# A flat loop over passes in TensorE's expert program, its three bodies in another order, and two small matmuls moved into the first gather

## The reference, cut to what matters

```python
def moe_ffn(h, w_router, b_router, w_exp_in, b_exp_in, w_exp_out, b_exp_out):
    logits = (t @ w_router + b_router).astype(jnp.float32)       # t: 256 x 1024, 32 experts
    top_val, top_idx = lax.top_k(logits, TOP_K)                  # 4 of 32
    gate_w = jax.nn.softmax(top_val, axis=-1)
...
        hb = xb @ w_exp_in[e] + b_exp_in[e]                      # 1024 -> 2 x 1024
        g = jnp.minimum(hb[:, :D_FF_2], SWIGLU_LIMIT)
        u = jnp.clip(hb[:, D_FF_2:], -SWIGLU_LIMIT, SWIGLU_LIMIT)
        a = g * jax.nn.sigmoid(SWIGLU_ALPHA * g) * (u + 1.0)
        return a @ w_exp_out[e] + b_exp_out[e]                   # 1024 -> 1024
...
    y = jnp.einsum('nk,nkd->nd', gate_w, y_slot)
```

## Time and profile before

| | before |
|---|---|
| runs, us | 1498.84, 1501.26, 1500.84 |
| median, us | 1500.84 |
| profiled execution, us | 1501.09 |
| its span, us | 1499.2 |
| granted TensorE clock, mean | 0.98 |
| experts | from about 550 us to the end |

### The profile page before, as it was taken

How to read it: one execution, slowest core, us unless ns; L and a number is a source line. 1 busy time by engine, 2 the same in 40 slices (tenths; PEclk the granted TensorE clock), 3 DMA queues, 4 the chain that set the end, 5 groups by cost and what they waited for, 6 DMA issues and landing times.

```text
span 1499.2 us, 25356 instructions
## 1 busy us (share of the span) xinstructions
PE 1336.5 (89%) x9367; PEld 800.2 (53%) x9368; DVE 449.1 (30%) x908; ACT 359.7 (24%) x691; POOL 139.4 (9%) x65
## 2 busy tenths in 40 slices
PE   7999999999999998988998888998889988889875
PEld 6455999988889863434343333343333333333432
DVE  1326687745543871101111110111011111111112
ACT  1234666545666621001000100010010001000101
POOL 0000112004776400000000000000000000000000
PEclk9999999999999999999999999999999999999997
DMA  9441366855344478999999999999999999999996
GB/s 339 151 136 56 112 187 189 323 192 176 135 166 169 167 319 363 428 424 428 426 422 425 428 427 425 425 409 427 425 425 428 410 426 427 427 427 424 410 427 259
DMA packets 113493, 494.35 MB, mean 330 GB/s; under 512 B 7617, under 2 KB 55089, under 8 KB 80465
## 3 DMA queue, kind: packets, MB, share of 16 engines
q1 hardware_dynamic: 111971, 491.50, 81.6%
q10 hardware_dynamic: 1486, 2.34, 0.5%
HBM read 492.76 MB, written 1.06 MB: 329 GB/s over the span
## 4 chain that ended last, share of the span: by engine, by line
PE 60%; DMA 31%; ACT 3%; DVE 3%; issue 2%; SPq 0%; DVEq 0%; ACTq 0%
DMA big_mem<-in_w_exp_in 26%; PE ps L983 15%; PE ps L1025 7%; PE ps L702 5%; PE ps L704 5%; PE ps L703 5%; DMA big_mem<-in_w_exp_out 5%; PE ps L530 4%; PE ps L966 3%; PE ps L674 2%; PE ps L726 1%; PE ps L728 1%; PE ps L727 1%; PE ps L1048 1%; PE ps L519 1%
## 5 line engine op out<-in xcount | busy, mean ns | idle before, releaser
L983 PE MATMUL ps<-big_mem,ring_mem 128*32 128x512 f32 (+1 forms) x2304 | 375.2, 628 | 68.7 <-DMA big_mem<-in_w_exp_in 68.7
L983 PEld LDWEIGHTS ps<-big_mem,ring_mem 128*32 128x32 f32 (+1 forms) x2304 | 111.2, 123 | 310.5 <-issue 196.9
L1025 PE MATMUL ps<-big_mem,x 128*32 128x256 f32 (+1 forms) x1888 | 182.3, 430 | 9.6 <-DMA big_mem<-in_w_exp_out 5.7
L702 PE MATMUL ps<-hT_hi,w_hi 128*128 128x256 f32 x600 | 171.1, 285 | 1.3 <-DVE hT_lo L1662 1.3
L704 PE MATMUL ps<-hT_hi,w_lo 128*128 128x256 f32 x600 | 169.7, 283 | 0.0
L703 PE MATMUL ps<-hT_lo,w_hi 128*128 128x256 f32 x600 | 169.7, 283 | 0.0
L966 PEld LDWEIGHTS ps<-ring_mem,h 128*128 128x128 f32 x1024 | 131.4, 197 | 59.9 <-issue 59.9
L966 PE MATMUL ps<-ring_mem,h 128*128 128x96 f32 x1024 | 148.7, 289 | 0.0
L2146 DVE TENSOR_SCALAR ring_mem<-ps 128x256 f32<-128x256 f32 (+1 forms) x36 | 18.7, 520 | 425.8 <-PE ps L983 425.8
L1562 ACT ACTIVATE ring_mem<-ring_mem 128x256 f32<-128x256 f32 (+1 forms) x36 | 17.7, 493 | 490.2 <-DVE ring_mem L2146 490.2
L1025 PEld LDWEIGHTS ps<-big_mem,x 128*32 128x32 f32 (+1 forms) x1888 | 70.4, 115 | 107.8 <-issue 64.7
(11 more groups left out here) (345 smaller groups left out, 1502.3 us busy)
## 6 DMA issues: line engine op xcount, KB each, us to landing
big_mem<-in_w_exp_in SPq DMA_DIRECT2D x128, 2048.0 KB, 22.7
big_mem<-in_w_exp_out SPq DMA_DIRECT2D x128, 1024.0 KB, 22.6
ring_mem<-in_w_in SPq DMA_DIRECT2D x15, 2048.0 KB, 7.8
ring_mem<-in_w_up SPq DMA_DIRECT2D x44, 512.0 KB, 5.0
ring_mem<-in_w_down SPq DMA_DIRECT2D x5, 2048.0 KB, 8.6
ring_mem<-in_w_out SPq DMA_DIRECT2D x4, 2048.0 KB, 8.4
ring_mem<-in_w_branch_a SPq DMA_DIRECT2D x1, 2048.0 KB, 7.5
ring_mem<-in_w_branch_b SPq DMA_DIRECT2D x1, 2048.0 KB, 7.5
```

What stands on the lines that cost most here:

```text
L702: mm(out, hi, x_hi, start=start, stop=False)
L983: last = mm(out, stationary, weights[:, f, w * q:w * (q + 1)] if m > XS else weights[:, :, w * q:w * (q + 1)], start=start, stop=stop)
L1025: last = mm(ps[m * q:m * (q + 1), 4 + at // XS, 0:w], aT[:, k % n, k // n, :], wout[:, k, w * q:w * (q + 1)], start=(k == 0), stop=(k == K ...
```

## The change

PE's loop over E experts with an inner loop over passes becomes one flat loop over at most MOST_PASSES = 32 + 1024 // 97 = 42 passes. Registers hold the place in the order and the number of landed transfers; `load_next_or_same` keeps them for an expert that has another pass. Behind the last expert `further[0, E]` is TRIO = 3, and a turn that finds 3 skips everything; with 32 passes here, ten turns are such. The bodies stand in the order 1, 0, 2 (`If_eq` at L1141, `If` at L1143 and L1145). On DVE the memset of all of `cnt` becomes two of one column each.

The two matmuls of the totals leave their place behind L944 and stand between the two halves of the first gather; where they were, `keep_busy(1, 7)` puts one 128x512 matmul whose result is not used.

```diff
--- before.py
+++ after.py
@@ -31,6 +31,7 @@
 TRIO = 3
 SLOTS = TRIO * XS
 PASSES = -(-SEQ // SLOTS)
+MOST_PASSES = E + SEQ * 4 // (SLOTS + 1)
 TURNS = E + -(-SEQ * 4 // SLOTS) + 1
 EARLY = 5
 GROUPS = (((0, XS),), ((0, 2 * XS),), ((0, 2 * XS), (2 * XS, XS)))
@@ -942,8 +943,7 @@
             mm(ps[:, 5, 0:E], tri, sel[:, 0, :], start=True, stop=True)
             mm(ps[:, 5, E:2 * E], ones, sel[:, 0, :], start=True, stop=False)
             mm(ps[:, 5, E:2 * E], tri, sel[:, 1, :], start=False, stop=True).then_inc(s["rank_ps"], 1)
-            mm(ps[:, 4, 0:E], ones, sel[:, 0, :], start=True, stop=False)
-            mm(ps[:, 4, 0:E], ones, sel[:, 1, :], start=False, stop=True).then_inc(s["rank_ps"], 1)
+            keep_busy(1, 7)
 
             def bias_out():
 
@@ -1056,6 +1056,8 @@
                 if t == 0:
                     pe.wait_ge(s["pick0_ready"], 1)
                 else:
+                    mm(ps[:, 4, 0:E], ones, sel[:, 0, :], start=True, stop=False)
+                    mm(ps[:, 4, 0:E], ones, sel[:, 1, :], start=False, stop=True).then_inc(s["rank_ps"], 1)
                     pe.wait_ge(s["picks_ready"], 1)
                     pe.wait_ge(s["h1_ready"], T)
                 for k in range(KD):
@@ -1106,39 +1108,51 @@
             extra_reg, more_reg, next_extra, next_more = (pe.alloc_register("pe_" + z) for z in ("extra", "more", "next_extra", "next_more"))
             pe.reg_mov(extra_reg, pe.value_load(further[0:1, 0, 0:1], min_val=0, max_val=TRIO - 1))
             pe.reg_mov(more_reg, pe.value_load(further[0:1, 1, 0:1], min_val=0, max_val=PASSES - 1))
-            nth_reg = pe.alloc_register("pe_nth")
-            for r in (next_extra, next_more, nth_reg):
+            nth_reg, place_reg, landed_reg, step, step_landed = (pe.alloc_register("pe_" + z) for z in ("nth", "place", "landed", "step", "step_landed"))
+            for r in (next_extra, next_more, nth_reg, place_reg, step, step_landed):
                 pe.reg_mov(r, 0)
-            with pe.Fori(0, E) as e:
-                landed_all = 16 * e + 16
-                extra = pe.snap(extra_reg, min_val=0, max_val=TRIO - 1)
-                more = pe.snap(more_reg, min_val=0, max_val=PASSES - 1)
-
-                def load_next():
-
-                    pe.wait_ge(s["order_ready"], 1)
-                    following = pe.value_load(order[0:1, bass.ds(e + 1, 1)], min_val=0, max_val=E)
-                    pe.reg_mov(next_extra, pe.value_load(further[0:1, 0, bass.ds(following, 1)], min_val=0, max_val=TRIO - 1))
-                    pe.reg_mov(next_more, pe.value_load(further[0:1, 1, bass.ds(following, 1)], min_val=0, max_val=PASSES - 1))
-
-                with pe.If(extra < 1):
-                    one_pass(GROUPS[0], landed_all, load_next)
-                with pe.If(extra > 0):
-                    with pe.If(extra < 2):
+            pe.reg_mov(landed_reg, 16)
+            with pe.Fori(0, MOST_PASSES):
+                extra = pe.snap(extra_reg, min_val=0, max_val=TRIO)
+                with pe.If(extra < TRIO):
+                    more = pe.snap(more_reg, min_val=0, max_val=PASSES - 1)
+                    place = pe.snap(place_reg, min_val=0, max_val=E - 1)
+                    landed_all = pe.snap(landed_reg, min_val=16, max_val=16 * E)
+
+                    def load_next():
+
+                        pe.wait_ge(s["order_ready"], 1)
+                        following = pe.value_load(order[0:1, bass.ds(place + 1, 1)], min_val=0, max_val=E)
+                        pe.reg_mov(next_extra, pe.value_load(further[0:1, 0, bass.ds(following, 1)], min_val=0, max_val=TRIO))
+                        pe.reg_mov(next_more, pe.value_load(further[0:1, 1, bass.ds(following, 1)], min_val=0, max_val=PASSES - 1))
+                        pe.reg_mov(step, 1)
+                        pe.reg_mov(step_landed, 16)
+
+                    def load_next_or_same():
+
+                        load_next()
+                        with pe.If(more > 0):
+                            pe.reg_mov(next_extra, TRIO - 1)
+                            pe.reg_add(next_more, more_reg, -1)
+                            pe.reg_mov(step, 0)
+                            pe.reg_mov(step_landed, 0)
+                        pe.nop()
+
+                    with pe.If_eq(extra_reg, 1):
                         one_pass(GROUPS[1], landed_all, load_next)
+                    with pe.If(extra < 1):
+                        one_pass(GROUPS[0], landed_all, load_next)
                     with pe.If(extra > 1):
-                        with pe.Fori(0, PASSES) as p:
-                            with pe.If(more >= p):
-                                one_pass(GROUPS[2], landed_all, load_next)
-                            pe.nop()
-                        pe.nop()
+                        one_pass(GROUPS[2], landed_all, load_next_or_same)
                     pe.nop()
+                    with pe.If_eq(nth_reg, E // 2):
+                        bias_out()
+                    pe.reg_add(nth_reg, nth_reg, 1)
+                    pe.reg_mov(extra_reg, next_extra)
+                    pe.reg_mov(more_reg, next_more)
+                    pe.reg_add(place_reg, place_reg, step)
+                    pe.reg_add(landed_reg, landed_reg, step_landed)
                 pe.nop()
-                with pe.If_eq(nth_reg, E // 2):
-                    bias_out()
-                pe.reg_add(nth_reg, nth_reg, 1)
-                pe.reg_mov(extra_reg, next_extra)
-                pe.reg_mov(more_reg, next_more)
 
 
         @block.scalar
@@ -2091,7 +2105,8 @@
                 first = v.tensor_scalar(moe["picks"][:, t, :], stay[:, IOTA:IOTA + SLOTS], ps[:, 5, E * t:E * t + 1], sel[:, t, 0:1], ALU.is_equal, ALU.mult)
                 first.then_inc(s["pick0_ready" if t == 0 else "picks_ready"], 1)
             shifted1(1).then_inc(s["h1_ready"], 1)
-            v.memset(cnt[:], 0.0)
+            v.memset(cnt[:, 0, E:E + 1], float(TRIO))
+            v.memset(cnt[:, 1, E:E + 1], 0.0)
             dve.wait_ge(s["rank_ps"], 2)
             link(v.tensor_copy(tokens[:], ps[:, 4, 0:E]))
             for i, step in enumerate((1, TRIO)):

```

## The result

The changed kernel takes 1505.17 us (median of 20 runs, 1502.57 to 1508.51), the kernel before 1502.04 (20 runs, 1498.47 to 1506.05). The ratio is 1.0022, with a 95% interval of 1.0014 to 1.0031: 3.3 us slower, between 2.1 and 4.7. The forecast was 1502.3 in a range of 1496.2 to 1506.0, so the time lies in the range and 2.9 us above the forecast, just past the 0.2% that I had called the same. It is above the narrower 1500.5 to 1504.5 that I had given the forecast itself. The profiled execution took 1505.05 us.

The account below looks back on a forecast made before the run. The prediction took the weight stream and its dry stretches after late PE restarts to bound the kernel. Terms +1.2 +4.8 -4.5 -0.3 summed to +1.2 on 1501.09, so 1502.3 us, range 1496.2 to 1506.0.

Parts of the forecast that it names:

- What bounds the kernel: Expert part: weight stream at 426 GB/s; PE costs time only where a late restart lets the DMA queue run dry.
- (a): Totals inside the gather: DVE copies them later, delaying PE's first expert matmul; +1.2 us, bounds 0.8 to 2.2.
- (b): First expert to second: a second long jump, over body 2, and a longer way to body 0; +4.8 us.
- (c): Exits of body 2: PE restarts sooner, perhaps at a higher clock, recovering dry stretches; -4.5 us, bounds -3 to -4.7.
- (d): The end: ten empty turns covered by the tail, 0; clock in the tail's first matmuls -0.3 us, bounds -1.5 to +0.5.
- rival 1: First to second expert: no second stall, since L1145's target comes with L1143's fetch; -3.0 us, 1498.1; chance 0.33.
- Rival 2: Gather and first two experts: both jumps pay in full and the low clock stays; +5.6 us, 1506.7; chance 0.17.
- Rival 4: Behind body 2: SP or the queue sets the dry stretch, so no gain there; 1504 to 1507; chance 0.05.
- rival 3: The end: empty turns outlast the tail; at 1.5 us per turn +4, 1506; sign: last branch after 1496; chance 0.04.

Follow-up runs that it names:

- e2: Kernel before with only the totals moved into the gather and the wide matmul in their place, loop unchanged; 1.0013 of the kernel before.
- e8: Changed kernel with 52 turns in place of 42, so twenty empty ones; 1.0041 of the kernel before.
- e9: Changed kernel with 150 instructions that only move later code added at the start of PE's program; 1.0027 of the kernel before.
- e3: Changed kernel without the wide matmul (`keep_busy(1, 7)`); 1.0025 of the kernel before.
- e1: Changed kernel's flat loop, bodies 1, 0, 2, but totals back in their old place and no wide matmul; 0.9994 of the kernel before.
- e5: Kernel before, nested loop and old gather, with only the bodies put in the order 1, 0, 2; 1.0002 of the kernel before.
- e12: e5 with 14 instructions more at the start of PE's program; 1.0016 of the kernel before.
- e11: Kernel before with only 150 instructions added at the start of PE's program; 1.0024 of the kernel before.
- e7: Flat loop, totals in old place, order 1, 0, 2, with an empty turn jumping over all bodies ahead of the first expert; 1.0011 of the kernel before.
- e6: Flat loop, totals in old place, bodies in the order 0, 2, 1; 1.0000 of the kernel before.
- e4: Flat loop, totals in old place, bodies in the old order 0, 1, 2; 0.9979 of the kernel before.

## Why the prediction was right, and where it was off

**What bounds the kernel** held: the stream runs at 423 to 427 GB/s wherever PE restarts in time, and the whole difference lies in three stretches around PE's restarts.

**(a) The totals**: taken +1.2 with bounds of 0.8 to 2.2, measured +2.8 (12.83 to 15.61, and 12.8 to 15.6 in e2 alone). The mechanism and the first term were right: DVE's copy came 1.2 us later, PE's first product 1.3. The term that was missing is the low clock: I had put it into the gather, from where the wide matmul took it away; it fell into the first product, where it cost 1.5 us. e2 shows it by itself. How much of the product it takes varies: from first product to first issue e8 has 5.85 us and e9 6.91, with the same code there. That the wide matmul costs nothing held; e3 shows it to be worth about 2 us of the first stretch.

**(b) Expert 0 to expert 1**: taken +4.8, measured +6.9 (+6.5 in e1). Two long branches, at L1143 and L1145, stood where the prediction had put them. Mis-sized is the second one's price, 4.2 against 5.55. I had made it cheaper because the queue dries up meanwhile, and that relief was there: the first code packet starts 1.30 us behind the branch, in place of 3.65 at L1143. What I missed is that L1145 has two code packets in it (588.5 and 588.8 us), where L1129, from which I had the price, has one (581.9); two cost 7.39 and 7.54 us under full stream. The rest is the longer way to body 0 and the low clock, which lasts from 585.3 to 598.9. One reason given was wrong although its result was right, which was luck. I took the bodies for some 100 and over 200 instructions; those are rows of a listing that folds repeated ones. The trace has some 386, 300 and 617 records of PE's queue in one pass of bodies 0, 1 and 2, and what made L1143 dear in this kernel was its place in it (e5 against e12), not its being a first jump under stream.

**(c) and (d)**: taken -4.8 together, measured -5.3 in the stretch to the end. All four exits of body 2 are without loss, and the clock behind them is 1.00, as the second half of (c) had it. The 3.3 us that the prediction has for 1.1 per exit leaves out the first exit's 0.3; it should be 3.6, and the term taken does not use it. The gain in an average run may be smaller: in e2, with the old loop, two of the four exits show no loss either (427 and 425 GB/s in 1170 to 1200 and 1380 to 1410), so what they cost varies within one and the same loop; that it depends on where the low clock falls is a guess. Ten empty turns took 0.73 us each and were covered; e8 shows the cover to be gone between ten and twenty.

**The rivals.** The second stall came (rival 1 is out). Rival 2, slower with both jumps in full and the clock against it, is nearest to what happened in (a) and (b), but (c) was recovered whole. Rival 4 is out by the windows. For rival 3 my sign was a last branch later than 1496, and it starts at 1498.9: the last pass ended 4.0 us later than before, and the ten turns took 7.3. The sign was badly chosen, since it did not move with the rest. That branch is still 4.3 us ahead of the span's end, and e8 shows that there was room behind it, so rival 3 is out as well.

The range held with the two mis-sized terms erring the same way: +3.3 us is almost three times the +1.2 forecast. The sum of +1.2 became +4.0 in the profiled execution and +3.3 in the ratio: 1.6 too little in (a), 2.1 too little in (b), 0.5 too much caution in (c) and (d), and 0.4 of variation ahead of the routing.

## What to carry to other kernels

A branch in a long unrolled loop can cost several us (3.7 to 7.5 here) the first time that it skips to code that has not come yet, and here once even on its second time. Look at the maximum of each branch line, not its median, and at what runs dry behind it; adding or reordering code anywhere ahead can switch such a cost on (14 instructions did here). Moving the cost ahead of the stream gains nothing if that stretch is on the path too. And a small result on which another engine's chain hangs (here the totals, for the counts, the gates and PE's registers) belongs ahead of the bulk of the work, even where PE has time for it later.

## What the runs showed of the hardware that I had not expected

- A long branch costs most of its price even on idle DMA queues: 3.66 us with one code packet in it (e11) and 4.64 to 5.02 with two (e7, e6), against 5.05 to 6.43 and 7.39 to 7.54 under the stream.
- Code is not kept for good by being fetched once: in e4 the same branch to the same target was long twice, 27 us apart, and 26 code packets came where e1 needed 24.
- One 128x512 matmul of 1.1 us in a gap of PE kept the clock at 2.4 GHz through the gather that followed (after, e2, e8, e9); without it the low clock lasted 13.7 us (e3).
- Runs of one kernel spread by 0.5% (1498.5 to 1506.1 before), and the stretch from the second issue to the end alone differs by 2.7 us between before and e2, which have the same loop. Single profiles of this kernel are compared by stretch, not by their span.
